# Down stage: turning y in 32x32 blocks on VectorE and placing it with on-chip transfers, and more identity turns in the prologue

## The reference

```
h = rmsnorm(x, g_mix_pre);  proj = h @ w_in                 # 1024 -> 4608
attention (block-sparse, T5 bias) || conv + RG-LRU          # gated and merged
x = x + rmsnorm(merged @ w_out, g_mix_post)
f = rmsnorm(x, g_ffn_pre)
g_, u_ = split(f @ w_gate_up)                               # 1024 -> 2 x 2816
x = x + rmsnorm((silu(g_) * u_) @ w_down, g_ffn_post)       # 2816 -> 1024, the down stage
```

## Time and profile before

| | us |
|---|---|
| median of 3 runs | 787.91 |
| the runs | 784.64, 787.91, 788.05 |
| profiled execution | 788.1 |
| its span | 786.3 |
| PE busy in the span | 771.3 (98%) |
| DVE busy | 478.5 (61%) |
| ACT busy | 357.5 (45%) |
| mean granted clock of TensorE | 0.989 of full |

### The profile page before, as it was taken

The page is one execution under the profiler, slowest core; times in us unless marked ns, Lnnn a source line. Parts: engine busy times, 40 slices in busy tenths (PEclk is TensorE's granted clock), DMA queues, the critical chain, the costliest instruction groups (busy, mean ns, idle before and its releaser), DMA issues.

```text
span 786.3 us, 16392 instructions
## 1 busy us (share of the span) xinstructions
PE 771.3 (98%) x6036; PEld 730.6 (93%) x6036; DVE 478.5 (61%) x747; ACT 357.5 (45%) x618; POOL 66.4 (8%) x152
## 2 busy tenths in 40 slices
PE   8999999999999999999999999999999999999996
PEld 6888999899899899987799999999999999999995
DVE  4655847746657634784568987778877784222223
ACT  6345535534625532343456555554555563223232
POOL 3511102102012010003000000000000010000000
PEclk7999999999999999999999999999999999999998
DMA  7645555456444124515461333332333143222312
GB/s 211 174 108 116 155 132 134 131 131 137 121 113 120 54 85 147 175 56 180 167 188 28 108 107 107 107 93 85 89 107 107 54 154 108 75 88 79 97 50 114
DMA packets 180737, 90.26 MB, mean 115 GB/s; under 512 B 48773, under 2 KB 174169, under 8 KB 180698
## 3 DMA queue, kind: packets, MB, share of 16 engines
q1 hardware_dynamic: 177886, 82.67, 37.6%
q0 software_dynamic: 2576, 6.45, 2.5%
q10 hardware_dynamic: 236, 0.61, 0.3%
HBM read 82.89 MB, written 6.81 MB: 114 GB/s over the span
## 4 chain that ended last, share of the span: by engine, by line
PE 96%; DVE 1%; ACT 1%; DMA 1%; issue 0%; DVEq 0%; SPq 0%; ACTq 0%
PE ps L917 34%; PE ps L1259 27%; PE ps L1324 17%; PE ps L1158 6%; PE ps L1228 3%; PE ps L1017 1%; PE ps L1031 1%; PE ps L1049 1%; DMA x_tok<-in_x_prompt_dram 1%; PE ps L939 1%; PE ps L1091 1%; PE ps L946 1%; PE ps L1166 1%; PE ps L1002 1%; PE ps L1062 1%; PE ps L1193 0%
## 5 line engine op out<-in xcount | busy, mean ns | idle before, releaser
L1872 DVE TENSOR_TENSOR w_lo<-w_raw,w_hi 128x1024 fp32r<-128x1024 f32 (+1 forms) x68 | 80.9, 1191 | 137.3 <-ACT w_hi L1401 137.0
L1401 ACT ACTIVATE w_hi<-w_raw 128x1024 fp32r<-128x1024 f32 (+1 forms) x68 | 70.0, 1030 | 126.2 <-PE ps L1324 82.6
L917 PE MATMUL ps<-xin_hi,w_hi 128*128 128x272 f32 x576 | 125.2, 296 | 1.6 <-DVE xin_lo L1895 0.9
L917 PE MATMUL ps<-xin_hi,w_lo 128*128 128x272 f32 x576 | 120.4, 288 | 0.0
L917 PE MATMUL ps<-xin_lo,w_hi 128*128 128x272 f32 x576 | 120.1, 288 | 0.0
L917 PEld LDWEIGHTS ps<-xin_hi,w_hi 128*128 128x128 f32 x576 | 90.3, 188 | 10.0 <-issue 7.6
L917 PEld LDWEIGHTS ps<-xin_lo,w_hi 128*128 128x128 f32 x576 | 91.0, 188 | 0.0
L917 PEld LDWEIGHTS ps<-xin_hi,w_lo 128*128 128x128 f32 x576 | 90.5, 189 | 0.0
L1324 PE MATMUL ps<-hid_hi,w_hi 128*128 128x272 f32 x352 | 76.0, 291 | 0.4 <-DVE hid_lo L2274 0.4
L1324 PE MATMUL ps<-hid_lo,w_hi 128*128 128x272 f32 x352 | 74.9, 287 | 0.0
L1324 PE MATMUL ps<-hid_hi,w_lo 128*128 128x272 f32 x352 | 74.9, 288 | 0.0
(11 more groups left out here) (337 smaller groups left out, 1750.4 us busy)
## 6 DMA issues: line engine op xcount, KB each, us to landing
w_raw<-in_w_in_dram SPq DMA_DIRECT2D x72, 256.0 KB, 3.3
g_raw<-in_w_gate_up_dram SPq DMA_DIRECT2D x40, 256.0 KB, 3.7
w_raw<-in_w_down_dram SPq DMA_DIRECT2D x40, 256.0 KB, 2.8
u_raw<-in_w_gate_up_dram SPq DMA_DIRECT2D x20, 256.0 KB, 3.0
e_raw<-in_w_gate_up_dram SPq DMA_DIRECT2D x20, 256.0 KB, 4.2
kc<-in_cache_k_dram SPq DMA_DIRECT2D x64, 64.0 KB
vc<-in_cache_v_dram SPq DMA_DIRECT2D x64, 64.0 KB
wo_raw<-in_w_out_dram SPq DMA_DIRECT2D x12, 256.0 KB, 4.3
```

What stands on the lines that cost most here:

```text
L917: mm = e.matmul(ps[:, bank + h, 0:HT], wt[:, kw, :], xt[:, kx, h * HT:h * HT + HT], start=first and wt is wh and xt is xh, stop=last and ( ...
L1401: e.activation((to or w_hi[s])[:, 0:k, :], w_raw[s][:, 0:k, :], ACT.Copy).then_inc(hi_done, count)
L1872: e.tensor_tensor(wl[:, 0:k, :], w_raw[s][:, 0:k, :], wh[:, 0:k, :].bitcast(F32), ALU.subtract).then_inc(lo_done, count)
```

## The change

1. Down stage. TensorE no longer transposes y of tiles 0 to 6, and ScalarE no longer copies these. Instead ScalarE writes `yg` in another order of the tokens (four Identity instructions for the former one, two of 256 elements read in PSUM's order and written with a stride of 32, two of 16), VectorE transposes `yg` in blocks of 32x32 into `yz` (one instruction of 128x544), and SyncE places each tile in `ytok` by 12 on-chip transfers (`move_y`: for each of 4 groups of 32 partitions, two of 32 x 256 elements for the prompt and one of 32 x 32 for the sample), in pieces of 32 elements. SyncE issues `move_y(m)` behind the loads of tile m+1 and ahead of those of tile m+2. Before it transposes tile m, VectorE waits until the transfers of tile m-2 have landed; before the final sums it waits for all.
2. The tokens of a token tile are now every second one of 256 instead of 128 in a row; `x1tok` is loaded and y_prompt stored by the same order (rows of 4 KB as before), and the last tile's transposes and norm sums read their columns with a step of two.
3. Prologue: 58 identity turns for 45 ahead of `x_T(0)`, and 4 new ones between `x_T(0)` and `x_T(1)`.
4. Two semaphores are merged into others: `g_in` into `rel_in` (so that `x_norm(0)` also waits for the bucket table and the relative bias) and `xs_in` into `row_in` (so that `x1_rows` waits for all 14 row transfers of GpSimd: g_post, g_ffn and the 12 small ones of the samples).

```diff
         def y_cols(buf, tt):
-            c0 = 2 * P if tt == TT else tt * P + (tt // 2) * TS
-            return buf[:, c0:c0 + (TS if tt == TT else P)]
+            if tt == TT:
+                return buf[:, 2 * P:2 * P + TS]
+            c0 = tt // 2 * (2 * P + TS)
+            return buf[:, c0:c0 + 2 * P].rearrange("p (n s) -> p s n", s=2)[:, tt % 2]
...
+            def move_y(m, s):
+                tile = bass.ds(m * P, P)
+                prompt = ytok[:, 0:TT, tile].rearrange("p t (d c) -> p t d c", c=BLK)
+                sample = ytok[0:TS, TT, tile].rearrange("p (d c) -> p d c", c=BLK)
+                count = e.to_reg(m + 1)
+                e.wait_ge(consts, C_ZERO)
+                e.wait_ge(y_turned, count)
+                for d in range(P // BLK):
+                    rows = slice(BLK * d, BLK * d + BLK)
+                    for h in range(2):
+                        c0 = h * (2 * P + TS)
+                        e.dma_start(prompt[:, 2 * h:2 * h + 2, d, :], yz[s][rows, c0:c0 + 2 * P]).then_inc(y_moved, 16)
+                    e.dma_start(sample[:, d, :], yz[s][rows, 2 * P:2 * P + TS]).then_inc(y_moved, 16)
             for c in range(3):
                 load_down(1, c, (3 + c) % 2)
+            move_y(0, 0)
             with e.Fori(1, KD // 2) as n:
                 for m2 in range(2):
                     for c in range(3):
                         load_down(n * 2 + m2, c, (m2 * 3 + c) % 2)
+                    move_y(n * 2 + (m2 - 1), 1 - m2)
...
-            turn(45)
+            turn(58)
             x_T(0)
+            turn(4)
             x_T(1)
-            e.wait_ge(rel_in, 32)
+            e.wait_ge(rel_in, 48)
...
                     down_steps(c, odd, ks, c == 0 and not tail, c == 2).then_inc(tile_done, 1)
-                    if c == 0 and between is not None:
-                        y_T(between, 1 - odd)
...
             def y_evacuate(m, s):
                 e.wait_ge(tile_done, m * 3 + (C_DOWN + 5))
-                e.activation(halves(yg[s][:, :]), two(D_PAIR[s]), ACT.Identity, scale=prm[:, bass.ds(m + 48, 1)])
                 e.wait_ge(ysq_used, m + 1)
+                for h in range(2):
+                    bank, c0, t0 = 2 * D_PAIR[s] + h, h * (2 * P + TS), h * HS
+                    e.activation(yg[s][:, c0:c0 + 2 * P].rearrange("p (b i) -> p i b", i=BLK),
+                                 ps[:, bank, t0:t0 + 2 * P].rearrange("p (i b) -> p i b", i=BLK),
+                                 ACT.Identity, scale=prm[:, bass.ds(m + 48, 1)])
+                    e.activation(yg[s][:, 2 * P + t0:2 * P + t0 + HS], ps[:, bank, (1 - h) * 2 * P:(1 - h) * 2 * P + HS],
+                                 ACT.Identity, scale=prm[:, bass.ds(m + 48, 1)])
                 e.activation(halves(ysq[:, :]), two(D_PAIR[s]), ACT.Square).then_inc(y_free, 1)
...
-            def y_square(m):
+            def y_square(m, s):
                 e.wait_ge(y_free, m + 3)
+                if not isinstance(m, int):
+                    e.wait_ge(y_moved, m * 192 - 176)
+                e.transpose(yz[s][:, :], yg[s][:, :]).then_inc(y_turned, 1)
                 e.wait_ge(ysq_used, m + 1)
                 e.tensor_tensor(yacc[:, :], yacc[:, :], ysq[:, :], ALU.add).then_inc(ysq_used, 1)
```

More of the change, by code:

```diff
@@ L305, in program @@
     ytok = put("ytok", [P, TT + 1, D], where=w)
+    yz = [put(f"yz{i}", [P, T], where=w) for i in range(2)]
     assert w[0] <= x1_at
@@ L456, in program @@
         y_free = sem("y_free")
+        y_turned = sem("y_turned")
+        y_moved = sem("y_moved")
         y_sq_last = sem("y_sq_last")
@@ L537, in y_cols, with token_rows @@
         def y_cols(buf, tt):
-            c0 = 2 * P if tt == TT else tt * P + (tt // 2) * TS
-            return buf[:, c0:c0 + (TS if tt == TT else P)]
+            if tt == TT:
+                return buf[:, 2 * P:2 * P + TS]
+            c0 = tt // 2 * (2 * P + TS)
+            return buf[:, c0:c0 + 2 * P].rearrange("p (n s) -> p s n", s=2)[:, tt % 2]
+        def token_rows(rows, tt):
+            first = tt // 2 * (2 * P) + tt % 2
+            return AP(rows.tensor, first * D, [[2 * D, P], [1, D]])
         def tile_of(buf, k, k0=0):
@@ L886, in _ @@
                 rows = slice(TS * g, TS * g + TS)
-                e.dma_start(xs[rows, :], xst[:, g * QW:(g + 1) * QW]).then_inc(xs_in, 16)
-                e.dma_start(gs_post[rows, :], AP(norm_mix_post.tensor, g * QW, [[0, TS], [1, QW]])).then_inc(xs_in, 16)
-                e.dma_start(gs_ffn[rows, :], AP(norm_ffn_pre.tensor, g * QW, [[0, TS], [1, QW]])).then_inc(xs_in, 16)
+                e.dma_start(xs[rows, :], xst[:, g * QW:(g + 1) * QW]).then_inc(row_in, 16)
+                e.dma_start(gs_post[rows, :], AP(norm_mix_post.tensor, g * QW, [[0, TS], [1, QW]])).then_inc(row_in, 16)
+                e.dma_start(gs_ffn[rows, :], AP(norm_ffn_pre.tensor, g * QW, [[0, TS], [1, QW]])).then_inc(row_in, 16)
             x_row(1)
@@ L1327, in down_steps, with down @@
                 return mm
-            def down(m, odd, between=None, tail=False):
+            def down(m, odd, tail=False):
                 for c in range(3):
@@ L1353, in _ @@
             with e.Fori(0, (KD - 2) // 2) as n:
-                down(n * 2 + 1, 1, n * 2)
-                down(n * 2 + 2, 0, n * 2 + 1)
+                down(n * 2 + 1, 1)
+                down(n * 2 + 2, 0)
             def norm_part(tts):
@@ L1864, in _ @@
                             (tp_free, 1), (mi_free, 1), (o_free, 1), (rg_done, 1), (kv_out, 160), (mix_free, 2),
-                            (y_free, 2), (ysq_used, 1), (yt_free, 1), (silu2, 2), (uh1_done, 2), (gh1_done, 2)):
+                            (y_free, 2), (ysq_used, 1), (yt_free, 1), (y_moved, 16), (silu2, 2), (uh1_done, 2), (gh1_done, 2)):
                 e.sem_inc(sem_, n)
@@ L2362, in y_tile @@
                 down_lo(n, odd, 2)
-                y_square(m)
+                y_square(m, odd)
             for k in range(EARLY, 16):
@@ L2386, in _ @@
                 e.wait_ge(y_inv, h + 1)
-                e.wait_ge(yt_free, KD + h + 1)
+                e.wait_ge(yt_free, h + 2)
+                e.wait_ge(y_moved, 192 * (KD - 1) + 16)
                 for tt in (0, 1) if h == 0 else (2, 3, TT):
```

27 lines of the change are left out of this document (9 added, 18 removed).

## The result

| | before | after |
|---|---|---|
| median, us | 787.91 | 803.81 |
| runs, us | 784.34 to 788.58 (5 runs) | 801.69 to 804.28 (5 runs) |
| ratio to before | | 1.0205 [1.0178, 1.0233] |
| profiled execution, its span | 788.1, 786.3 | 802.24, 800.1 |
| mean granted clock | 0.989 | 0.988 |

The change makes the kernel about 2% slower; the forecast was 783.7, with a range up to 791.5. The ratio compares the five runs of each made together on one chip, and the 13.8 us between the two spans are what the traces have to explain.

A forecast was written before the change was run, and what follows sets the result against it. The prediction took TensorE, 96% of the chain that ended last, to bound the kernel. From 788.1 us it took 3.9 for transposes and 3.3 for identity turns, added 2.8 for a load stall: 783.7 us, range 780.4 to 791.5.

The forecast's parts named there:

- The transposes, -3.9: Down stage: seven tiles lose their TensorE transposes, 0.56 us each, 3.9 us gained if nothing takes their place.
- What takes their place, +2.8: Down stage: SyncE's 12 placing issues delay load (m+2,0) beyond its slack, 0.47 us for each of six tiles, 2.8 us lost.
- first rival: Down stage, load (m+2,0): SyncE's 12 issues cost over 0.62 us each; 790.2 us at 0.67, 796 at 0.75; chance 0.18.
- slack of 8.14 us: Down stage: how much later load (m+2,0) could come before TensorE waits; 8.14 us, against a forecast delay of 8.61.
- how it would fail furthest: Down stage: the 128-byte pieces hold up the queue itself, so that loads land later than 2.7 us.
- The identity turns, -3.3: Prologue: added turns keep the clock at 2.4 GHz, first projection matmul at 19.2 instead of 22.5, 3.3 us gained.
- fourth rival: Prologue: the clock falls despite the added turns, gain 0; 787.0 us, or 784.8 half of the way; chance 0.18.
- What was costed at nothing: Merged-semaphore waits at x_norm(0) and x1_rows, ScalarE's longer evacuation, and the tail's strided reads (0 to 1 us): taken as 0.

The follow-up runs named there:

- e3: The changed kernel with tile m's placing transfers later in SyncE's order, behind loads (m+2,0) and (m+2,1); 784.50 us, ratio 0.9964 to before.
- e8: The changed kernel with the placing behind loads (m+2,0) and (m+2,1) and before's identity turns (45 and none); 782.55 us, ratio 0.9966 to before.
- e11: e3 with the cached keys loaded in 512-byte rows (wrong key order); 780.64 us, ratio 0.9933 to before.
- e9: The kernel before with the change's identity turns and the cached keys loaded in 512-byte rows; 784.11 us, ratio 0.9977 to before.
- e6: The changed kernel with all 12 transfers a tile, the 8 large ones cut to 1/8 of their content; 800.6 us, one run.
- e7: The changed kernel with tile m's placing transfers between loads (m+2,0) and (m+2,1); 787.12 us, ratio 1.0004 to before.
- e1: The kernel before with only the change's identity turns (58 for 45, and 4 new); 789.46 us, ratio 1.0017 to before.
- e10: The kernel before with only the cached keys loaded in 512-byte rows, no added turns; 783.93 us, ratio 0.9976 to before.
- e2: The changed kernel without its added identity turns (45 and none, as before); 798.21 us, ratio 1.0125 to before.
- e4: The changed kernel with the placing transfers issued by GpSimd instead of SyncE; 785.77 us, ratio 0.9986 to before.
- e5: The changed kernel with half of the placing transfers, 6 a tile in the same place; 787.35 us, one run.

## Why the prediction was wrong, step by step

**The transposes, -3.9: right.** The period without a loop is 16.58 us (e3, e8) against 17.13, and e11 stands 3.5 us under e9.

**What takes their place, +2.8: the step that failed.** It measured +18.7: in TensorE's time, 12.8 of waits and 5.9 of clock. Three things were wrong in it.
- The issue. I took 0.58 us from start to start, from the weight loads' 0.56 (same loop, also a register in the address); it is 0.78. The row it should have been nearest to was the store of K in 128-byte pieces, 0.67, which I set aside because it has twice the pieces. e6 shows that size and pieces hardly count (0.63 against 0.64 us). By my own figure of 0.12 us a tile for each 0.01 us above 0.54, 0.78 gives a stall of 2.9 us a tile, 17 in all, and a time of 798, further out on the first rival's line. So this one figure accounts for most of the miss in size, but that it comes so near is partly luck: the sum had an equal stall before each of the tiles 2 to 7, and measured were 3.91, 0.50, 4.24, none, 3.47 and 0.64.
- The load that matters. I gave a slack of 8.14 us to load (m+2,0) and wrote that the next loads have over 5 us each. Chunk (m+2,1) is different: its copy stands ahead of the evacuation of tile m+1 on ScalarE, and the evacuation is what starts the next placing. A late (m+2,1) delays the next placing, which makes the following loads late again. I followed the delay to TensorE and stopped there, instead of following it once round to where it began. e7, where (m+2,0) is ahead of the placing and only (m+2,1) is behind it, has 17.35 and not 16.58: a loop closes through this load too.
- The landing. 2.7 us is the landing of a load that goes out in a pair. Held back by the placing, four go out in a row, and the last takes 5.06, 5.27 and 3.88 in the three periods where it lies on the chain. The prediction named this as how it would fail furthest, but for another reason (pieces in the queue); e3 has the same pieces, a median landing of 2.9 and 3.4 at the longest. (Over the whole down stage of before the longest is 4.3, not the 3.3 of the earlier trace rows.)

The Trainium skill, "DMA: Bandwidth & Descriptors", section "Issuing engines are not separate DMA queues", was weighed against this step: by it the issue is small beside the transfer. Here a placing transfer lands in 2.1 us and SyncE is kept 0.78 us by each, twelve times in a row, and this serial part is what the loop consists of. The trace disagrees as said, only more than I thought.

**The first rival had the right sign and place**, a load behind costly issues on SyncE, and 796 at 0.75 us an issue. It had 0.18. What it lacked is the loop, and the clock: here the stalls of 3.5 to 4.2 us are followed by a stretch at 1.2 GHz. I priced stalls by their length alone, in a kernel whose prologue had shown me falls behind an empty TensorE.

**The identity turns, -3.3: right where I looked, lost further on.** 18.22 against a forecast 19.2; the clock stayed up in after, and e9's ten runs lie in one group (the one at 785.78 stands 1.7 over the others' median, with the same mean clock, 0.997, as they; what it lost is not known). The step that failed is the sentence that later waits of this stage follow TensorE itself. In the attention stage they follow SyncE, which issues without a pause; e1 gives the gain back in a wait of 2.4 us at 113 us and the slow clock behind it, e9 and e11 keep it with cheaper issues. The size had a second fault: the 3.3 was subtracted in full, though it is only won in executions whose clock would have fallen, and e10's clock held without the turns in eight of ten. What I wrote of the lowest run of before, that it looks like one in which the clock did not fall, is borne out by e10: its two groups are 4.3 us apart, with mean clocks of 0.997 and 0.989.

**The fourth rival, the clock falls all the same: open in part.** I set against it that each fall seen had an empty TensorE before it. e3's fall at 14.7 us has only 0.23 us of that (and 0.46 five microseconds earlier), and comes behind the narrow bias matmuls, as the rival said; it is one profile of nine. The Trainium skill, "TensorE: Matmul & The Clock Gate", Part 4, has it that transposes don't count for the clock gate. By that the turns could change nothing, and e8 and e10, whose clock holds without them, show how little one profile proves. The comparison in numbers leans against the rule, eight of nine profiles with the turns at 1.00 against two of four without, but thirteen profiles are too few to decide. More direct is that in e3 the clock came back at 18.1 us, when TensorE had run only transposes since 14.7.

**What was costed at nothing** held: the strided writes (ScalarE's four Identity and the Square end 2.89 us after the start of the copy ahead of them, forecast 3.17, and SyncE begins 3.98 after it, forecast 4.13), VectorE's transpose (0.745, forecast 0.73), x_norm(0) began 0.06 us later, and the tail is within half a microsecond.

**What stays open:** what sets the loop at 19.07 or 19.68 us (e2 against after), and what decides, in the original form of the cached-key loads, whether the wait for the scores is 0.3 us (after), 0.6 (e4), 4.0 (e7) or 4.5 (e5). Both are sensitive to when SyncE comes to a load, but no run fixed that alone. What makes the prologue's clock fall in one execution and not in the next is open too. Twelve transfers merged into fewer were not tried.

## What to carry to other kernels

A wait written into an in-order queue is a link; follow it forward through every engine until it either reaches TensorE with slack or comes back to itself, and compare the length of the closed loop with the period of the bound engine: here 19.4 to 20.4 us against 16.6, and with the waiting transfers put two loads later in the same queue a tile took 16.58. Put transfers that wait for results behind the loads that feed the next step, or on a queue with nothing else to do, and count issues, not bytes. Time gained at the start of a kernel is only gained if every later stage is bound by the engine that gained it.

## What the runs showed of the hardware that was not expected

- The issue of an on-chip to on-chip transfer with 128-byte pieces takes SyncE 0.60 us for 32 pieces and 0.64 for 256 (after); cut to 32 pieces the second kind still takes 0.63 (e6). With the register work around it, it is 0.78 from start to start. On GpSimd it takes 0.52 and 0.73 (e4). A weight load takes 0.37 in the same stage.
- Loads of cached keys in 128-byte pieces keep the issuing queue 1.02 us (median, up to 3.3), in 512-byte rows 0.35.
- The last of four weight transfers of 256 KB issued in a row landed in 3.7 to 5.3 us (after, e2), against a median of 2.7 for the pairs of before.
- The clock fell in one execution behind narrow matmuls with only 0.23 us of idle time just before it (e3), and the same kernel's clock fell in some executions and not in others (e10: 788.2 us at a mean clock of 0.989, 783.9 at 0.997).
- TensorE waits of 3.9 and 4.2 us were followed by stretches at 1.2 GHz (clock 0.66 and 0.52 over the next 5 us), a wait of 0.5 us was not; 132 matmuls took 19.18 instead of 16.59. Around 2.3 us it went both ways (e2: 2.36 followed by a clock of 0.50, 2.33 by 1.00).
